# A decoder layer with expert retrieval: a gather ring of seven places, v rows two slots behind, the sample's heads routed in one pass, the new state in the other half buffer

## What is computed

```python
def peer_ffn(hn, wq, subkeys, u, v):            # 8 heads, 128*128 experts
    ...
        q = (xc @ wq).reshape(PEER_CHUNK, PEER_HEADS, 2, PEER_DKEY // 2)
        s = jnp.einsum('chpd,hpkd->chpk', q, subkeys)
        s1, i1 = lax.top_k(s[:, :, 0], PEER_TOPK)        # 16 of 128
        s2, i2 = lax.top_k(s[:, :, 1], PEER_TOPK)
        cand = (s1[..., :, None] + s2[..., None, :])     # 16 x 16
        cidx = (i1[..., :, None] * PEER_KEYS + i2[..., None, :])
        top, sel = lax.top_k(cand, PEER_TOPK)
        expert = jnp.take_along_axis(cidx, sel, axis=-1)
        g = jax.nn.softmax(top, axis=-1)
        act = jax.nn.gelu(jnp.einsum('cd,chkd->chk', xc, u[expert]))
        return jnp.einsum('chk,chkd->cd', g * act, v[expert])
```

## Time and profile before

| | |
|---|---|
| median of three runs | 2360.34 us (2345.57, 2360.34, 2369.19) |
| the profiled execution | 2349.1 us, span of the core 2347.3 us |
| granted TensorE clock, mean | 0.84 |
| TensorE matmul busy | 1799.1 us, 77% of the span |
| VectorE busy | 1398.5 us, 60% |
| ScalarE busy | 970.5 us, 41% |
| GpSimd busy | 633.8 us, 27% |
| DMA | 696.49 MB, mean 297 GB/s; 562.07 MB of it by the gathers |

### The profile page before, as it was taken

How to read it: one execution, slowest core, us unless ns; L and a number is a source line. 1 busy time by engine, 2 the same in 40 slices (tenths; PEclk the granted TensorE clock), 3 DMA queues, 4 the chain that set the end, 5 groups by cost and what they waited for, 6 DMA issues and landing times.

```text
span 2347.3 us, 21073 instructions
## 1 busy us (share of the span) xinstructions
PE 1799.1 (77%) x6297; PEld 936.9 (40%) x6297; DVE 1398.5 (60%) x3401; ACT 970.5 (41%) x3156; POOL 633.8 (27%) x560
## 2 busy tenths in 40 slices
PE   7999997587777458876667888767878868888645
PEld 3443654444334134432435545424333343354311
DVE  1120131497666869867665788667766636655794
ACT  2000222354444345454445554444545524544333
POOL 0000000132333323333332322333345523222222
PEclk9999798778889678988898789888988969978677
DMA  5133617388999788999999878999999979998755
GB/s 180 52 92 86 228 36 262 136 329 324 374 352 334 277 315 319 368 391 363 359 357 391 318 304 339 378 364 354 370 333 345 368 297 350 379 367 336 303 216 224
DMA packets 133962, 696.49 MB, mean 297 GB/s; under 512 B 22728, under 2 KB 32296, under 8 KB 65656
## 3 DMA queue, kind: packets, MB, share of 16 engines
q0 software_dynamic: 78016, 562.07, 62.5%
q1 hardware_dynamic: 55832, 133.07, 16.1%
HBM read 683.84 MB, written 15.44 MB: 298 GB/s over the span
## 4 chain that ended last, share of the span: by engine, by line
PE 30%; DMA 30%; DVE 19%; issue 13%; POOL 5%; ACT 3%; SPq 0%; DVEq 0%; POOLq 0%; ACTq 0%
DMA arena<-in_peer_uv,expert 28%; PE bank L916 10%; PE bank L1490 6%; DVE arena L2421 5%; DVE arena L2433 5%; POOL arena L868 4%; PE bank L1190 2%; PE bank L1226 1%; PE bank L1127 1%; PE bank L1175 1%; PE bank L1313 1%; PE bank L1110 1%; PE bank L1460 1%; DVE arena L2197 1%; PE bank L980 1%
## 5 line engine op out<-in xcount | busy, mean ns | idle before, releaser
L868 POOL DMA_INDIRECT arena<-in_peer_uv,expert x512 | 587.1, 1147 | 1658.8 <-DVE arena L2433 911.5
L1490 PE MATMUL bank<-arena 128*128 128x512 f32 (+1 forms) x1376 | 813.6, 726 | 255.7 <-ACT arena L1874 241.6
L2421 DVE CUSTOM_DVE_ANT_0 arena<-arena 128x1024 f32<-128x1024 f32 x520 | 636.4, 1224 | 503.4 <-DMA arena<-in_peer_uv,expert 480.0
L1490 PEld LDWEIGHTS bank<-arena 128*128 128x128 f32 (+1 forms) x1376 | 286.9, 228 | 599.5 <-ACT arena L1874 291.9
L1861 ACT ACTIVATE arena<-arena 128x1 f32<-128x1 f32 x520 | 104.9, 202 | 892.7 <-DVE arena L2421 875.9
L916 PE MATMUL bank<-arena 128*128 128x512 f32 (+3 forms) x560 | 227.5, 565 | 0.0
L2433 DVE SCALAR_TENSOR_TENSOR arena<-arena 128x1024 f32<-128x1024 f32 x176 | 225.4, 1280 | 0.0
L1866 ACT ACTIVATE arena<-arena 128x1 f32<-128x1 f32 x520 | 201.2, 387 | 17.3
L1864 ACT ACTIVATE arena<-arena 128x1 f32<-128x1 f32 x520 | 193.8, 373 | 0.2
L1874 ACT ACTIVATE arena<-arena 128x128 f32<-128x128 f32 (+1 forms) x344 | 137.8, 401 | 31.8 <-ACT arena L1866 0.4
L916 PEld LDWEIGHTS bank<-arena 128*128 128x128 f32 (+1 forms) x560 | 93.6, 169 | 133.0 <-issue 127.9
(11 more groups left out here) (275 smaller groups left out, 2024.2 us busy)
## 6 DMA issues: line engine op xcount, KB each, us to landing
arena<-in_w_out SPq DMA_DIRECT2D x10, 2048.0 KB, 15.8
arena<-in_peer_wq SPq DMA_DIRECT2D x10, 2048.0 KB
arena<-in_w_in SPq DMA_DIRECT2D x6, 2048.0 KB, 8.9
arena<-in_w_mq SPq DMA_DIRECT2D x5, 2048.0 KB
arena<-in_w_mo SPq DMA_DIRECT2D x5, 2048.0 KB
arena<-in_peer_uv,expert POOLq DMA_INDIRECT x512
sc_proj<-arena SPq DMA_DIRECT2D x3, 1676.0 KB, 5.4
arena<-sc_proj SPq DMA_DIRECT2D x3, 1676.0 KB
```

Source lines behind the costliest of these rows:

```text
L868: pool.indirect_dma_start(out=ring[:, p % RING, :], out_offset=None, in_=a["peer_uv"], in_offset=bass.IndirectOffsetOnAxis(ap=idx, axis=0) ...
L1490: ins = pe.matmul(banks[6 + half][0:R, :], diag[:, n % NDIAG, 0:R], ring[:, k, D + half * 512:D + (half + 1) * 512], start=(p == FIRST_PE[ ...
L2421: dve.tensor_tensor_reduce(out=ring[:, k, 0:D], in0=ring[:, k, 0:D], in1=x, scale=GELU_B, scalar=0.0, op0=ALU.mult, op1=ALU.add, accum_out ...
```

## The change

The ring gets a seventh place, and VectorE adds a v row two slots behind its dot instead of three. The space for the seventh place comes from the sample's own columns: its residual row, its normed row and its routing results had a third place beside the two that the tiles alternate between; they now lie in the space of the sample's mixer and are loaded again or made there. The memory rows lie elsewhere, and the limit of that part of the memory is moved.

The sample's routing is one pass. Its 64 pairs of head and token stand on 64 partitions: the queries are put on the block diagonal of a padded matrix, eight matmuls gather the scores of all heads in one bank, one `route_head` over 12 slots from slot 484 finds the experts, and a multiply with a mask and two matmuls with a 0/1 matrix spread the result to the layout that the gathers want.

The sample's new state is made in the other half buffer, so that the projection of tile 2 no longer shares its space; its load stands before the two stores, and waits that the stores are done now stand elsewhere. In the sample's group, the loads of w_out stand behind the wait for its stored rows.

```diff
-RING = 6
+RING = 7
-PE_LAG, V_LAG = 2, 3
+PE_LAG, V_LAG = 2, 2
 def head_start(gh):
-    return {0: -40, ...}.get(gh, 16 * gh - 32) if gh < PT * H else 481 + 3 * (gh - PT * H)
+    return {0: -40, ...}.get(gh, 16 * gh - 32) if gh < PT * H else 484
 def head_span(gh):
-    return {1: 7, 2: 9}.get(gh, 16) if gh < PT * H else 3
+    return {1: 7, 2: 9}.get(gh, 16) if gh < PT * H else 12
+PASSES = PT * H + 1
-        h = base.take(3, D)
+        h = base.take(2, D)
-        hn3 = ar.take(3, D)
+        hn3 = ar.take(2, D)
-        s_state = half_w[0].rearrange("p (d e) -> p d e", d=HD)
-        s_prod = half_w[1].rearrange("p (d e) -> p d e", d=HD)
+        s_state = half_w[1].rearrange("p (d e) -> p d e", d=HD)
+        s_prod = half_w[0].rearrange("p (d e) -> p d e", d=HD)
...
+        q_pad = ar.take(H, 64)
+        cat_s = ar.take(D)
+        h_s = ar.take(D)
+        hn_own = cat_s
...
             sp.wait_ge(proj_done, NCH * NT)
-            for t in range(2):
-                sp.dma_start(mem_x[:, t, :], a["mem_prompt"][0, t * P:(t + 1) * P, :]).then_inc(mem_in, 16)
...
             sp.wait_ge(rows_stored, ROWS_STORED)
+            for t in range(2):
+                sp.dma_start(mem_x[:, t, :], a["mem_prompt"][0, t * P:(t + 1) * P, :]).then_inc(mem_in, 16)
...
             def output_weights(t):
...
+                if t == 2:
+                    sp.wait_ge(s_stored, 16)
                 sp.dma_start(w8[:, 4:8], w_out[:, 4:8]).then_inc(w_out_in[1], 16)
...
             sp.dma_start(out["s_state"][0]..., s_state[0:64]).then_inc(s_stored, 16)
+            sp.dma_start(pj, sc_proj[2]).then_inc(proj_loaded, 16)
             sp.wait_ge(s_ret_ready, 1)
             sp.dma_start(sc_cat[0]..., s_rows[0:64, S_Y, :]).then_inc(scratch_stored, 16)
-            sp.wait_ge(s_stored, 16)
             sp.wait_ge(scratch_stored, 32)
-            sp.dma_start(pj, sc_proj[2]).then_inc(proj_loaded, 16)
             output_weights(2)
...
             sp.dma_start(sc_cat[1]..., s_o[0:64, 3, :]).then_inc(scratch_stored, 16)
+            sp.wait_ge(scratch_stored, 48)
+            sp.dma_start(h_s[0:DB, :], x_rows(SAMPLE)).then_inc(x_again, 16)
             sp.dma_start(w8[:, 0:4], w_out[:, 0:4]).then_inc(w_out_in[0], 16)
             sp.dma_start(w8[:, 4:8], w_out[:, 4:8]).then_inc(w_out_in[1], 16)
             sp.wait_ge(scratch_stored, 48)
...
             def route_keys():
-                for n in range(2, 4 * NT):
+                for n in range(2, 4 * PT):
                     yield head_start(2 * n) - 3
                     key_scores(*divmod(n, 4))
+                yield head_start(PT * H) - 3
+                bank = claim(2)
+                pe.wait_ge(qp_ready, H * NT)
+                for hh in range(H):
+                    ins = pe.matmul(bank[0:64, 0:256], q_pad[:, hh, :], skT[:, hh, :], start=(hh == 0), stop=(hh == H - 1))
+                ins.then_inc(ks_done, 1)
...
-            pe.wait_ge(routed, H * NT)
-            pe.transpose(bank[:, 0:DB], expert_f[0:DB, :], ident[0:DB, 0:DB])
-            pe.transpose(bank[:, DB:2 * DB], gate_f[0:DB, :], ident[0:DB, 0:DB]).then_inc(rt_done, 1)
+            pe.wait_ge(spread_ready, 1)
+            for x in range(2):
+                ins = pe.matmul(bank[:, x * DB:(x + 1) * DB], spread_s[0:64, x].rearrange("p h k -> p (h k)"),
+                                own_row[0:64, :], start=True, stop=True)
+            ins.then_inc(rt_done, 1)
...
                     act.wait_ge(cat_ready, t)
+                    if t == 2:
+                        act.wait_ge(s_ret_ready, 1)
...
                 copy_rowsT(grp.xT, 0, DB)
+                act.wait_ge(set_ready, 6)
...
                     if s == 11:
+                        if t == 2:
+                            dve.wait_ge(scratch_stored, 32)
                         dve.wait_ge(ret_done, t + 1)
...
-                yield 12
-                dve.wait_ge(hnT_done, 2 * (NT + 2))
+                yield 37
+                dve.wait_ge(subT_done, 2)
                 dve.memset(skT, 0.0).then_inc(set_ready, 1)
...
             def route_head(gh):
                 gi, head = divmod(gh, H)
-                R = rows_of(gi)
+                R = P if gi < PT else 64
...
             def routes():
-                for gh in range(1, H * NT):
+                for gh in range(1, PASSES):
...
+                dve.wait_ge(routed, PASSES)
+                tt(spread_s[0:64], picked_s[0:64]..., own_head[0:64, :]..., ALU.mult).then_inc(spread_ready, 1)
...
+                dve.wait_ge(x_again, 16 * 3)
                 residual(grp, out_done, out_added, 3)
+                dve.memset(q_pad, 0.0).then_inc(set_ready, 1)
```

More of the change, by code:

```diff
@@ L181, in trunk_kernel @@
         cmp_neg = base.take(PT, H)
+        own_head = base.take(H)
+        own_row = base.take(DB)
         own_neg = base.take(256)
@@ L239, in trunk_kernel @@
         pick = ar.take(2, TOPK)
-        expert_f = ar.take(SLOTS)
-        gate_f = ar.take(SLOTS)
+        picked_s = ar.take(2, TOPK)
+        spread_s = ar.take(2, H, TOPK)
         gate_s = ar.take(DB)
         gate_t = ar.take(2, SLOTS)
-        assert ar.at - base.at <= 21600
-        MEM_OFF = 21600
+        assert ar.at - base.at <= MEM_OFF, ar.at - base.at
         ar = base.part(MEM_OFF, XW - MEM_OFF)
@@ L290, in trunk_kernel @@
         w0_q = base.part(4096, KC * D).take(KC, D)
+        mem_x = base.part(KC * D + 4096, 2 * D).take(2, D)
         mT = base.part(HN3, 2048).take(KC, NMEM)
-        mem_x = base.part(HN3 + 2048, 2 * D).take(2, D)
-        memn_gain = base.part(HN3 + 4096, D).take(D)
-        sub_k = base.part(QTP, 1024).take(H, P)
+        memn_gain = base.part(HN3 + 2 * D, D).take(D)
+        sub_k = base.part(HN3 + 3 * D, 1024).take(H, P)
         mk = base.part(SHEAD + 64, 1024).take(2, 512)
@@ L357, in trunk_kernel @@
         ms_probsT = ar.take(2, 32)
-        qT_ps = ar.take(H, DB)
+        q_pad = ar.take(H, 64)
+        ar.take(64)
+        q_pad_diag = base.part(ar.at - base.at - 576, 576).take(H, 72)
+        cat_s = ar.take(D)
+        h_s = ar.take(D)
+        hn_own = cat_s
         mem_piece = [v.rearrange("p (b n) -> p b n", b=4) for v in half_w]
@@ L588, in load_chunk @@
                     sp.dma_start(w_buf[:, b, :, 0:n], w_in[:, :, c0:c0 + n]).then_inc(w_in_loaded[b], 16)
[L590 to L593 removed]
+            for t in (0, 1):
+                sp.dma_start(h[:, t, :], x_rows(t)).then_inc(x_in, 16)
+            for t in (2, 3, SAMPLE):
+                sp.dma_start(proj[t][0:rows_of(t), 0:D], x_rows(t)).then_inc(x_in, 16)
             for dst, src in first_loads:
@@ L1740, in routes @@
             def routes():
-                for gh in range(1, H * NT):
-                    if gh >= 4 and gh % 2 == 0:
+                for gh in range(1, PASSES):
+                    if gh == PT * H:
+                        yield head_start(gh) - 2
+                        act.wait_ge(ks_done, 4 * PT + 1)
+                        act.wait_ge(routed, 2 * (4 * PT - 1))
+                        act.activation(s_head[0:64, 0, 0].rearrange("p y n -> p (y n)"), banks[2][0:64, 0:256], ACT.Copy
+                                       ).then_inc(ks_ready, 1)
+                    elif gh >= 4 and gh % 2 == 0:
                         yield head_start(gh) - 2
@@ L2442, in add_sum @@
                 for half in range(2):
-                    hv = h[0:R, hslot(t), half * 512:(half + 1) * 512]
+                    hv = groups[t].h[0:R, half * 512:(half + 1) * 512]
                     tt(hv, hv, banks[6 + half][0:R, :], ALU.add).then_inc(sum_added, 1)
```

50 lines of the change are left out of this document (27 added, 23 removed).

## The result

The changed kernel takes 2163.4 us (median of four runs, 2138.4 to 2174.0) against 2361.8 us before: ratio 0.9133, 95% interval 0.9037 to 0.9229. Ratios here compare mean times of executions in the faster of two states, which leaves out the one of 2174.0 us, so they are not quotients of the medians. Measured again beside three other kernels it took 2152.2 us, ratio 0.9176 (0.9136 to 0.9216). The forecast was 2254 with a range from 2195 to 2312; the direction is right, and the gain is about twice what was forecast. The time is near that of the rival "more than I forecast" (2170), which had 0.10.

A forecast was written before the change was run, and what follows sets the result against it. The long stretch was held by how many gathers may be under way, the last stretch by VectorE's work. 59 + 40 - 2 - 2 = 95 us off 2349.1 gave 2254; range 2195 to 2312.

The forecast's parts named there:

- more than I forecast: Rival, chance 0.10: transfers at 0.99 throughout, 138 + 45 - 4 = 179 us gained, time 2170.
- as was asked for: Signs of being right: GpSimd's v-row wait under 400 us from 911.5, long stretch's DMA share 0.94 or more.
- The term for ring and lag: Long stretch, 452 to 2162 us: more gathers under way, 595 MB at 366 GB/s; 59 us gained, bounds 15 and 138.
- The two discounts: Off the long stretch's 84 us: 18 for TensorE close behind in two stretches, 7 for another wait around 1925.
- The upper bound: Long stretch with everything at 0.99, 378.6 GB/s: 1572 us, a gain of 138 us.
- In the 0.99 stretch the share has no room: Argument for rival "nothing more to fetch faster", chance 0.17: long stretch gains only 15 us, time 2298.
- The sample's pass: Last stretch, 2162 to 2303 us: seven passes of 8.8 us fewer, transfers then longest; 40 us gained.
- what the forecast named for its lower bound: Last stretch: only 10 us gained if TensorE's queries for the sample stop the ring anyway.
- The earlier projection: Third tile's projection loaded about 28 us before needed; up to 9.8 us of waiting go, nothing added to the sum.
- The costs: Subkey matrix clearing 2 us, sample's output projection loads 2 us (bounds 0 and 5); memory rows and last gathers nothing.
- a sign that it is wrong: Wrong if GpSimd mostly still waits for VectorE, VectorE waits for ScalarE's coefficients, or TensorE's waits for weights appear.
- The slower rival: Chance 0.04, halved from 0.08: weight loads come late behind more gathers, TensorE stops; 24 loads at 5 us each, 2374.

The follow-up runs named there:

- cheap users: Changed kernel with dots over 64 of 1024 columns, v rows and their matmuls over 64 columns of each kind: 2129.2 us, ratio 0.9076.
- eight: Changed kernel with eight routing passes of the sample's scores on 64 partitions in place of one, three slots each from slot 484: 2193.0 us, ratio 0.9360.
- r6v3: Changed kernel with six ring places and v rows three slots behind, as before; all else as changed: 2316.2 us, ratio 0.9866.

## Why the prediction was wrong in size and right in kind

1. **What bounds the kernel: right.** GpSimd and VectorE waited for each other for lack of gathers under way. In the changed kernel GpSimd's wait for the v row is under 400 us and the share of the long stretch over 0.94, as was asked for. Undoing ring and lag brings back 888.8 us of GpSimd's wait and 1696 us of stretch.
2. **The term for ring and lag: this step failed.** It said "I take 59": 595 MB at 366 GB/s, 84 us less, then 18 off for TensorE and 7 for the stop around 1925. The whole stretch lost 144.5 us, 130 of them by ring and lag. The error has two parts. The 366 GB/s that the small ring reached over 200 us was taken as what the transfers can do, but in those 200 us (1450 to 1650 of the kernel before) the old loop was still in force, and GpSimd waited 125.1 of them for the v row:

```profile
POOL arena L868 <- DVE arena L2433: 125.1, 23, 9.8
```

The changed kernel averages 380 over the whole stretch, and 386 over slots 336 to 408. At 380, the 595 MB take 1566 us (the measured time, written as a rate). That is 60 of the 85 us that were missing.
3. **The two discounts: wrong too.** TensorE, busy 0.86 of slots 336 to 408, did not hold them: that stretch and slots 240 to 280 gave 15.8 and 20.4 us, 36 in all, where 35.7 was reckoned at 366 GB/s and half of it credited. The stop around the sample's output projection stayed (20.9 us for the rows, 78.4 us for slots 408 to 424 at 0.69), but the mean rate of the stretch already includes it. These 25 us are the rest. Slots 240 to 280 stay at 0.91 and 361 GB/s with VectorE, not TensorE, busiest (121.82 of 130.9 us); what holds them was not tried.
4. **The upper bound was the better estimate.** 1572 us at 0.99 throughout was the stated bound; 1566 was measured, at a share of 0.96, for the reason in the last section. "In the 0.99 stretch the share has no room" was right as a limit and misplaced as a rival: over the long stretch the limit lies near 388 GB/s (cheap users, and `eight`) and not near 351 (595 MB in the 1695 us of its lower bound).
5. **The sample's pass: right in size, in part by luck in what bounds it then.** 40 us forecast; 38.0 in the profile, 41 by the run with eight passes, at 8.4 us for a pass against 8.8. The forecast had the transfers as the longest, at 369 GB/s throughout. Of the changed kernel's rows below, from slot 480 on, the first third runs at 257 GB/s with TensorE busy 33.10 of 33.10 us, and the rest at 396. Against 369 the one loses 10 us and the other wins 5, so that the dot of slot 511 still came near the 100 us of the forecast (100.5 behind that of slot 480, before 140.5). So the share does not reach 0.9 (0.80 to slot 512, as shown above).

```profile
2016.90:2050.00 33.10, 33.10 (x139) 22.90 (x140) 11.76 (x26) 9.84 (x40) 5.48 (x5) 0.72 0.66 257
2050.00:2118.60 68.60, 47.94 (x84) 18.38 (x82) 45.11 (x87) 34.66 (x123) 30.56 (x25) 0.85 0.96 396
```

In that first third stands what the forecast named for its lower bound, TensorE's queries for the sample: VectorE stops for them between slots 480 and 490, by way of ScalarE, which also copies them. The first row below is a v row waiting for its coefficient, the second the pass waiting for its scores.

```profile
2040.31 1.28 DVE L2473 SCALAR_TENSOR_TENSOR arena<-arena 128x1024 f32<-128x1024 f32 x1 [4.44 <-ACT arena L1897]
2046.54 0.48 DVE L2224 MAX8 arena<-arena 64x8 f32<-64x128 f32 x2 [4.95 <-ACT arena L1770]
```

6. **The earlier projection: its wait went, as forecast**, 9.83 us before and 12 in the run that undoes it. With the edits other than ring and lag it makes up the 14 us of r6v3's long stretch at most (from slot 104 to 128 r6v3 took 78.4 us and the kernel before 89.5); in the time of the changed kernel it does not show.
7. **The costs: small, as forecast.** TensorE's wait for the sample's rows went from 19.15 to 20.9 us, where 2 more were reckoned. The first dot comes at 450.9 us, where it was 452.1, so the later clearing of the subkey matrix has no cost that shows. VectorE waits for coefficients 5.3 us in all, 4.4 of them in the place shown above; the prediction had named such a wait as a sign that it is wrong, and it is one, of this size.
8. **The slower rival: its mechanism is there and is cheap.** TensorE has 40 us of waits that it did not have before (17.8, 9.4, 7.6, 3.4 for loads in the rows above, and 2.1 for a store), a sign of being wrong by the prediction's own list; by its count 95 were needed to undo the gain it forecast. With ring and lag undone they are absent. The weights do land later: by the profile page's part on DMA issues w_mq takes 21.4 us from issue to landing in r6v3 and 26.0 in the changed kernel. The Trainium skill, "DMA: Bandwidth & Descriptors", section "Queues, rings and completion order", has the engines take the queues in turn, by which I had halved this rival. That a load on another queue then loses nothing was my step from it, and these rows do not agree with that step; the turn-taking itself shows in no row. Since the gathers run on during these waits, the net is what the stretch shows.

## What to carry to other kernels

When two engines wait for each other round a ring of buffers, count in slots how long a place is open for its transfer; here one place more and one slot less of holding were worth about the same, and the one that costs no memory (a shorter lag) should be tried first. Before a good stretch's rate is taken as the ceiling of such a loop, look whether the loop is still in force there. The 366 GB/s fell short of the 144.5 us by 60; the best row before, 392 over 50 us, would give 1518 us and overshoot by 48. The likeliest case lay between them, and not at the lower. Once the transfers are near their limit, removing a wait of 10 us may leave no trace in the total.

## What was not expected of the hardware

The gathers move the same bytes in less engine time when more of them are under way. The gather queue's line of the page, first of the kernel before, then of the changed one (the share is of 16 engines over the span):

```profile
q0 software_dynamic: 78016, 562.07, 62.5%
```

```profile
q0 software_dynamic: 78016, 562.07, 64.8%
```

62.5% of 2347.3 us are 1467 us, 64.8% of 2162.7 are 1401, 4.5% less for the same 78016 packets. With six places and three slots it is 1468 (63.5% of 2311.6), with six and two 1433 (64.8% of 2212.1), with seven and three 1421 (65.0% of 2186.9), with cheap users 1398 (65.7% of 2127.2). So a busy share is no fixed measure of the room left: 0.91 went with 348 GB/s, 0.96 with 380, which is 382 and 396 GB/s for a share of one, and an estimate that extends the rate by the share alone comes out too low. The changed kernel also holds 380 GB/s over 1566 us and 401 over 71.7 us, above the 358 GB/s that the prediction quoted from the Trainium skill, "DMA: Bandwidth & Descriptors", section "Specifications"; that figure is half of what two cores share, here one core runs, and the measurement decides. Why the packets take less time was not tried.
